# Triangular inverses with 16x16 diagonal blocks on VectorE, and cross-attention head by head, in a two-block transformer kernel

## The chip, the cores and the metric

One core of a Trainium2 chip runs the whole kernel in one launch. The metric is the device time of one execution in microseconds (us), as the median of several runs; smaller is better. Engines: TensorE (PE), VectorE (DVE), ScalarE (ACT), GpSimd (POOL) and SyncE (SP), which only issues loads and stores here.

## The reference

Two transformer blocks are applied to 256 tokens of width 2048, all in float32. The first one (a forgetting attention, an mLSTM cell, a mixture of very many small experts) isn't touched. The second one is: RMS norm, an input projection, a gated delta rule on 8 heads of 128, an RWKV-7 recurrence on 16 heads of 64, an output projection, a cross-attention with 4 heads to 256 memory tokens, and a feed-forward net. The change touches three places in it.

The delta rule solves, for each head and chunk of tokens, a unit lower triangular system:

```
a_strict = where(strict, (kb @ k^T) * decay, 0)
sol = triangular_solve(a_strict + I, rhs, lower=True)
```

The RWKV-7 recurrence is a scan over tokens in the reference; the kernel computes it in chunks of 128 tokens, and needs the inverse of a unit lower triangular 128x128 matrix for each head and chunk as well. The cross-attention:

```
scores = einsum('bshd,bmhd->bhsm', q, k) * 128 ** -0.5
probs = softmax(scores, axis=-1)
o = einsum('bhsm,bmhd->bshd', probs, v) @ wo
```

## The kernel before

Each engine has one written-out program, and the programs meet only at semaphores (`wait_ge` and `then_inc`). There is no planner: the order of the statements of an engine's program is the order of its work. In the helper class `Own`, `tell` raises a semaphore when an instruction is done, and `done` raises it and also waits for it on the same engine. SyncE streams weight tiles of 128x2048 into a ring of four slots. ScalarE rounds each slot to its high part (`high`, L1136), VectorE subtracts to get the low part (`low`, L2057), and TensorE does three passes over the parts (L2312 to L2314).

**Inverses.** There are three calls of the inversion, c = 0 (delta rule) and c = 1, 2 (the two halves of the RWKV heads). Each call inverts 16 matrices of 128x128 at once, handled in four groups q of four matrices. `Ti` holds the inverse and `Tt` its transpose. `inverse_dve` (L1605) sets both to I minus the entries inside the 2x2 diagonal blocks. Then come levels l = 1 to 5, which join blocks of 2 to 4, 4 to 8, 8 to 16, 16 to 32 and 32 to 64. In a level GpSimd (`inverse_pool`, L555) masks out the entries between the pairs of blocks (L558). TensorE (`inverse_pe`, L2446) multiplies them by Ti in `first(q)` (L2460), ScalarE (`inverse_act`, L818) copies the result to SBUF (L828), and TensorE multiplies by Tt on either side in `then(q)` (L2468, L2470). VectorE subtracts the products from Ti and Tt (L1620, L1622). TensorE's order is first 0, first 1, then 0, first 2, then 1, first 3, then 2, then 3. A last step joins 64 to 128 with 64x64 products (L2486, L2494; VectorE L1628), and updates only Tt.

For c = 0 the matrix AM is built by 16 VectorE operations (L1757) and a masking product (L1760). TensorE turns AM, and also the decay-weighted scores that L1763 writes; ScalarE copies both out (L922, L925). VectorE weights the turned K (L1767). When Tt is done, VectorE builds the right-hand side RH (L1775), and TensorE goes on (L2601). For c = 1 and 2, VectorE masks 16 products (L1990) into GR, ScalarE adds an off-diagonal part (L1099), TensorE turns the 16 matrices (L2763), and VectorE copies them out (L1994) before it starts. TensorE goes on at L2775.

**Cross-attention.** TensorE computes the scores of all heads (L2651). VectorE takes the row maxima of all in one instruction (L1848) and scales them. ScalarE does eight exponentials with sums (L990). VectorE multiplies by the reciprocal sums (L1852). TensorE turns the weights (L2657), ScalarE copies them out (L995), TensorE multiplies by the values (L2662), ScalarE copies the result (L998) and rounds it to the high part (L1000), VectorE forms the low part (L1854). Only then do ScalarE and VectorE split the first slot of the output projection `xo`, and TensorE goes on with it.

Of the kernel before, what the change touches and what calls it, by code (L numbers as in the profile page):

```python
# [17 lines left out]
F32 = mybir.dt.float32  # L18
# [7 lines left out]
P = 128  # L26
# [34 lines left out]
for _name, _units, _dv, _ac in UNITS:  # L61
# [16 lines left out]
                     ("dec_out", 1), ("atn_out", 4), ("at_out", 4), ("v_tok", 4), ("qs_out", 8), ("od_sq", 1),  # L78
                     ("od_root", 1), ("xa_exp", 1), ("xa_pt", 4), ("xo_high", 1)],
    "tensor_steps": [("gate_mm", 1), ("cumsum_mm", 1), ("r_mm", 1), ("qk_mm", 2), ("k_turned", 1), ("sm_turned", 2),  # L80
                     ("cp_mm", 4), ("num0_mm", 4), ("inter_mm", 4), ("num1_mm", 4), ("scores_mm", 8), ("hk_turned", 1),
                     ("l2_mm", 3), ("gc_mm", 1), ("dec_mm", 4), ("kk_gram", 4), ("qk_gram", 4), ("qd_turned", 4),
                     ("a_turned", 4), ("v_turned", 4), ("kd_turned", 1), ("xa_mm", 1), ("xa_turned", 4), ("xa_o", 4)],
# [4 lines left out]
                     ("dn_diag", 1), ("dec_arg", 1), ("a_ready", 1), ("qd_ready", 4), ("kd_ready", 1), ("xa_max", 1),  # L88
                     ("xa_p", 1)],
# [38 lines left out]
def build(nc, a, out):  # L128
    ctx = ExitStack()
    with ctx:  # L130
# [111 lines left out]
        OMU, OKA, SEL8 = SM[:, 192:218], SM[:, 218:226], SM[:, 226:240]  # L242
        SS, RS, RSTD = SM[:, 2:4], SM[:, 4:6], SM[:, 6:8]
# [106 lines left out]
        AOFS = [av(14336, 4, 4, P), av(33554, 4, 4, P), av(33554, 4, 4, P)]  # L350
        M1B = av(35602, 2, 4, P)

# [24 lines left out]
        RAM, RTI, RTT = av(0, 16, P), av(2048, 16, P), av(4096, 16, P)  # L377
# [176 lines left out]

        def inverse_pool(pool, c, At):  # L555
# [36 lines left out]
        def stage2_pool(pool, o):  # L592
# [5 lines left out]

            pool.wait_ge(*nth("at_out", 4))
            inverse_pool(pool, 0, AT_)  # L600
# [10 lines left out]
            for hf in range(2):  # L611
                pool.wait_ge(ev["decayed"], hf + 1)
                pool.wait_ge(ev["gram_out"], 16 * hf + 16)
                inverse_pool(pool, 1 + hf, GR[:, :, 0, :])
# [203 lines left out]
        def inverse_act(act, c):  # L818
# [4 lines left out]
            with act.Fori(1, 6, 1) as l:  # L823
                for q in range(4):
                    g = 4 * l + (24 * c - 4 + q)
# [4 lines left out]
            for q in range(4):  # L830
                g = 24 * c + 20 + q
# [5 lines left out]
        def stage2_act(act, o, half, freed, norm, high, highs):  # L837
# [82 lines left out]
            for n in range(4):  # L920
                act.wait_ge(*nth("qd_turned", n + 1))
                o.tell(nc.scalar.copy(flat(ATN)[:, BLK * n:BLK * (n + 1)], PP[:, n // 2, n % 2, :]), ev["atn_out"])  # L922
            for n in range(4):
                act.wait_ge(*nth("a_turned", n + 1))
                o.tell(nc.scalar.copy(flat(AT_)[:, BLK * n:BLK * (n + 1)], PQ[:, n, :]), ev["at_out"])  # L925
# [4 lines left out]
            inverse_act(act, 0)  # L930
# [55 lines left out]
            highs("xq", 0, (2, 3))  # L986
            freed(nc.scalar.copy(flat(XQ[:, 2:4, :]), half("xq", 0)))
            act.wait_ge(*nth("xa_max", 1))
            for n in range(8):
                ins = nc.scalar.activation(XP[:, n // 2, n % 2, :], PQ[:, n // 2, (n % 2) * T:(n % 2 + 1) * T], ACT.Exp,  # L990
                                           scale=QK_SCALE, bias=XST[:, 0, n:n + 1], accum_out=XST[:, 1, n:n + 1])
            o.tell(ins, ev["xa_exp"])
            for n in range(4):
# [611 lines left out]
        def inverse_dve(dve, o, v, c, A, At, Ti, Tt, ready):  # L1605
# [10 lines left out]
            with dve.Fori(1, 6, 1) as l:  # L1616
# [7 lines left out]
                for q in range(4):  # L1624
                    update(q)
# [1429 lines left out]
```

## Time and profile before

| | before |
|---|---|
| median of 3 runs | 3991.14 us (3989.09 to 3993.26) |
| the profiled execution, its own time | 3994.92 us |
| its span on the core | 3991.7 us |
| TensorE busy | 3712.8 us |
| VectorE busy | 2413.6 us |
| ScalarE busy | 1502.7 us |
| GpSimd busy | 157.9 us |

The three inversions lie at about 2565 to 2635, 2740 to 2814 and 2930 to 3004 us of the span, and the cross-attention at 3195 to 3221. A busy share is an average over the whole kernel; whether an instruction counts is read from the chain of waits in its stretch. TensorE instructions in fp32 appear as two records each where they are products, and as one where they are transposes.

### The profile page before, as it was taken

The page shows a single profiled execution, that of the slowest core. Times are in us where ns is not written, and L with a number is a line of the kernel's source. Part 1 is how long each engine was busy: PE and PEld are TensorE (multiplying, and loading weights), DVE is VectorE, ACT ScalarE, POOL GpSimd, SP SyncE. Part 2 cuts the span into 40 slices and gives each one's busy share as a digit, 9 for nine tenths or more (in the row PEclk, how much of TensorE's full clock was granted, in tenths as well). Part 3 has the DMA queues.
Part 4 walks back from the last instruction along what each step waited for, and adds up shares of the span by engine and source line. Part 5 has one row for each costly group of instructions (what it writes and reads, how often), then busy time and mean ns, then how long its engine had stood idle before and what let it go on. Part 6 is the DMA issues. An engine that isn't in the chain of part 4 may idle for free.

```text
span 3991.7 us, 54679 instructions
## 1 busy us (share of the span) xinstructions
PE 3712.8 (93%) x22418; PEld 3305.0 (83%) x22418; DVE 2413.6 (60%) x2621; ACT 1502.7 (38%) x1294; POOL 157.9 (4%) x159
## 2 busy tenths in 40 slices
PE   8996899999999999999999999777787969999998
PEld 8985699999988888888888989576676868888887
DVE  3544547977677766666666644456465445566656
ACT  3333333445434333433344433322222343343334
POOL 2000000000000000000000000122121000000000
PEclk8998899999999999999999999798787989999999
DMA  4451444556767765565554544000012425555554
GB/s 178 174 191 51 148 160 174 204 191 221 264 227 244 252 219 200 200 205 200 200 200 155 184 152 156 10 22 32 22 43 106 169 86 189 189 189 189 189 188 148
DMA packets 122889, 650.35 MB, mean 163 GB/s; under 512 B 10737, under 2 KB 43889, under 8 KB 49553
## 3 DMA queue, kind: packets, MB, share of 16 engines
q1 hardware_dynamic: 116224, 620.20, 44.5%
q0 software_dynamic: 6544, 28.44, 1.9%
q8 instruction: 89, 1.46, 0.2%
q14 instruction: 32, 0.25, 0.0%
HBM read 620.81 MB, written 27.79 MB: 162 GB/s over the span
## 4 chain that ended last, share of the span: by engine, by line
PE 87%; DVE 9%; ACT 2%; issue 1%; DMA 1%; DVEq 0%; ACTq 0%; POOL 0%; SPq 0%; PEldq 0%
PE pairs L2312 19%; PE pairs L2313 19%; PE pairs L2314 19%; PE quad L2357 12%; PE quad L2358 6%; DVE w_low L2057 2%; PE quad L2468 1%; PE pairs L2470 1%; PE quad L2398 1%; PE quad L2460 1%; PE quad L2865 1%; ACT w_high L1136 0%; PE quad L2703 0%; DVE arena L1940 0%; PE quad L2788 0%
## 5 line engine op out<-in xcount | busy, mean ns | idle before, releaser
L2057 DVE TENSOR_TENSOR w_low<-ring,w_high 128x2048 fp32r<-128x2048 f32 (+1 forms) x547 | 1253.2, 2292 | 926.8 <-ACT w_high L1136 926.3
L1136 ACT CAST w_high<-ring 128x2048 fp32r<-128x2048 f32 (+1 forms) x547 | 1039.2, 1901 | 1737.4 <-PE pairs L2314 1276.0
L2312 PE MATMUL pairs<-x_t,w_high 128*128 128x256 f32 x2592 | 745.4, 288 | 19.3 <-DVE w_low L2057 10.7
L2313 PE MATMUL pairs<-x_t,w_high 128*128 128x256 f32 x2592 | 738.8, 285 | 0.0
L2314 PE MATMUL pairs<-x_t,w_low 128*128 128x256 f32 x2592 | 738.8, 285 | 0.0
L2357 PE MATMUL quad<-x_t,w_high 128*128 128x512 f32 x1984 | 703.0, 399 | 9.9 <-DVE w_low L2057 9.9
L2312 PE MATMUL pairs<-w_high,act_high 128*128 128x512 f32 x1568 | 613.8, 391 | 10.2 <-DVE w_low L2057 6.5
L2313 PE MATMUL pairs<-w_low,act_high 128*128 128x512 f32 x1568 | 612.9, 391 | 0.0
L2314 PE MATMUL pairs<-w_high,act_low 128*128 128x512 f32 x1568 | 612.4, 391 | 0.0
L2358 PE MATMUL quad<-x_t,w_low 128*128 128x256 f32 x1984 | 558.1, 281 | 0.0
L2312 PEld LDWEIGHTS pairs<-x_t,w_high 128*128 128x128 f32 x2592 | 502.5, 194 | 22.0 <-DVE w_low L2057 11.8
L2313 PEld LDWEIGHTS pairs<-x_t,w_high 128*128 128x128 f32 x2592 | 502.6, 194 | 0.0
L2314 PEld LDWEIGHTS pairs<-x_t,w_low 128*128 128x128 f32 x2592 | 502.1, 194 | 0.0
L2357 PEld LDWEIGHTS quad<-x_t,w_high 128*128 128x128 f32 x1984 | 373.6, 188 | 102.6 <-DVE w_low L2057 10.3
L2358 PEld LDWEIGHTS quad<-x_t,w_low 128*128 128x128 f32 x1984 | 375.9, 189 | 1.1
L2312 PEld LDWEIGHTS pairs<-w_high,act_high 128*128 128x128 f32 x1568 | 295.6, 188 | 74.1 <-issue 12.0
L2314 PEld LDWEIGHTS pairs<-w_high,act_low 128*128 128x128 f32 x1568 | 295.5, 188 | 61.9
L2313 PEld LDWEIGHTS pairs<-w_low,act_high 128*128 128x128 f32 x1568 | 295.7, 189 | 60.1
L1429 DVE TENSOR_TENSOR x_res<-x_res,pairs 128x1024 f32<-128x1024 f32 x128 | 156.1, 1220 | 80.1 <-PE pairs L2314 79.1
L2312 PE MATMUL pairs<-w_high,x_t 128*128 128x512 f32 (+1 forms) x472 | 180.7, 383 | 9.5 <-DVE w_low L2057 9.5
L2313 PE MATMUL pairs<-w_low,x_t 128*128 128x512 f32 (+1 forms) x472 | 181.2, 384 | 0.0
L2314 PE MATMUL pairs<-w_high,x_t 128*128 128x512 f32 (+1 forms) x472 | 180.7, 383 | 0.0
(526 smaller groups left out, 3487.8 us busy)
## 6 DMA issues: line engine op xcount, KB each, us to landing
ring<-pu SPq DMA_DIRECT2D x128, 1024.0 KB, 4.9
ring<-pv SPq DMA_DIRECT2D x128, 1024.0 KB, 4.9
ring<-f SPq DMA_DIRECT2D x128, 1024.0 KB, 4.7
ring<-win SPq DMA_DIRECT2D x48, 1024.0 KB, 4.9
ring<-dn SPq DMA_DIRECT2D x32, 1024.0 KB, 4.9
ring<-rw SPq DMA_DIRECT2D x24, 1024.0 KB, 4.8
ring<-wout SPq DMA_DIRECT2D x16, 1024.0 KB, 4.9
ring<-wq SPq DMA_DIRECT2D x16, 1024.0 KB, 4.9
```

The lines of the kernel that those rows point to most:

```text
L1136: nc.scalar.copy(WH[s % 2][:, 0:w], flat(ring[s])[:, 0:w]).then_inc(ev["split_high"], 1)
L1429: v.tensor_tensor(X[:, :, cols], X[:, :, cols], PP[:, (UNIT0["peer"] + nb) % 2], ALU.add).then_inc(ev["dve_free"], 1)
L2057: v.tensor_tensor(WL[s % 2][:, 0:w], flat(ring[s])[:, 0:w], WH[s % 2][:, 0:w].bitcast(F32), ALU.subtract).then_inc(ev["split_low"], 1)
L2312: mm(out, stat[0], mov[0], start=start, stop=False, skip_group_check=True)
L2313: mm(out, stat[0], mov[1], start=False, stop=False, skip_group_check=True)
L2314: return mm(out, stat[1], mov[0], start=False, stop=stop, skip_group_check=True)
L2357: mm(PQ[:, m, :], wh[:, k, cols], XTB[:, :, kt, :], start=(kt == 0), stop=False, skip_group_check=True)
L2358: ins = mm(PQ[:, m, 0:T], wl[:, k, cols], XTH[:, kt, :], start=False, stop=(kt == KT - 1), skip_group_check=True)
L2398: ins = mm(PQ[:, 2 + b, t * P:(t + 1) * P], A0[:, b, t, :], B0[:, b, t, :], start=True, stop=True)
L2460: ins = mm(PQ[:, q % 2, m * P:(m + 1) * P], AOFS[c][:, q, m, :], Ti[:, 4 * q + m, :], start=True, stop=True)
L2468: mm(PQ[:, 2 + q % 2, m * P:(m + 1) * P], Tt[:, 4 * q + m, :], M1B[:, q % 2, m, :], start=True, stop=True)
L2470: ins = mm(PP[:, q % 2, 0, m * P:(m + 1) * P], M1B[:, q % 2, m, :], Tt[:, 4 * q + m, :], start=True, stop=True)
```

## The change

For c = 0, 1, 2 the 2x2 start and levels 1 to 3 go. A new VectorE function `substitute` inverts all 128 diagonal blocks of 16x16 (16 matrices with 8 blocks) at once, with one block in each partition: it transposes the 32x32 diagonal blocks in such a way that a partition holds two 16x16 blocks, picks one of them by a per-partition factor (EVEN16, built once), inverts by joining blocks of 2, 4, 8 and 16 inside the partition, and transposes the inverse and its transpose back into Ti and Tt, two of four row groups itself and two by a ScalarE copy. TensorE then does the level from 16 to 32 (its entries masked by ScalarE), the level from 32 to 64, where the product for Ti covers only the upper left 64x64, and the last step as before. Ti, Tt and the off-diagonal tile are cleared beforehand, by GpSimd (memset) or ScalarE (copies of zeros). For c = 0 the LS product goes, the weighting of K moves to ScalarE, and the weighting of the right-hand side moves ahead of the levels; for c = 1, 2 the turned copy of the matrices goes. The cross-attention is done head by head, and the split of xo's first slot moves ahead of it. The diff, cut to its core:

```diff
         def inverse_pool(pool, c, At):
-            for l in range(1, 6):
-                for q in range(4):
-                    if l >= 2:
-                        pool.wait_ge(ev["inv_m1"], 4 * l + (24 * c - 5 + q))
-                    between(q, LVA[:, l:l + 1, :])
+            for q in range(4):
+                pool.wait_ge(ev["inv_m1"], 12 * c + 4 + q - 1)
+                between(q, LVA[:, 5:6, :])
...
+            pool.wait_ge(used, SLOT0["out2"])
+            nc.gpsimd.memset(flat(AOFS[0]), 0.0).then_inc(ev["inv_off"], 1)
+            nc.gpsimd.memset(TTI, 0.0).then_inc(ev["inv_off"], 1)
+            pool.wait_ge(*nth("dec_mm", 4))
+            nc.gpsimd.memset(TI, 0.0).then_inc(ev["inv_off"], 1)
...
+        def block_cells(T_, g):
+            return T_[32 * g:32 * g + 32, :, 32 * g:32 * g + 32].rearrange("p m (b j) -> p j b m", b=2)
+
+        def inverse_act(act, o, c, At, Ti, Tt):
...
+            for g in range(4):
+                r, cols = slice(32 * g, 32 * g + 32), slice(32 * g + 16, 32 * g + 32)
+                ins = nc.scalar.mul(AOFS[c].rearrange("p q m s -> p (q m) s")[r, :, cols], At[r, :, cols], EVEN16[r, 0:1])
+            o.tell(ins, ev[f"off16_{c}"])
+            if c == 0:
+                act.wait_ge(ev["inv_off"], OFF0[c] + 3)
+            else:
+                nc.scalar.copy(Ti, rep(TRI[:, 0:P], 16))
+                o.done(nc.scalar.copy(Tt, rep(TRI[:, 0:P], 16)), ev[f"cleared{c}"])
+            for n, T_ in enumerate((Ti, Tt)):
+                act.wait_ge(*nth(f"blocks_turned{c}", n + 1))
+                for g in range(2):
+                    ins = nc.scalar.copy(block_cells(T_, g), BLKS[32 * g:32 * g + 32, :].rearrange("p (j b m) -> p j b m", j=16, b=2))
+                o.tell(ins, ev[f"blocks_out{c}"])
...
+        def substitute(dve, o, v, c, A, turned, Ti, Tt):
+            C, N = COEF[c], INV16[c]
+            o.tell(v.memset(N, 0.0), o.order)
+            for g in range(4):
+                r = slice(32 * g, 32 * g + 32)
+                ins = v.transpose(BLKS[r, :].rearrange("p (c b i) -> p c b i", c=16, b=2),
+                                  A[r, :, 32 * g:32 * g + 32].rearrange("p m (b c) -> p c b m", b=2))
+            o.done(ins)
+            C3 = C[:, 0:256].rearrange("p (c i) -> p c i", c=16)
+            pair = BLKS.rearrange("p (c b i) -> p c b i", c=16, b=2)
+            o.done(v.tensor_scalar(C3, pair[:, :, 0, :], MINUS16[:, 0:1], None, ALU.mult))
+            o.tell(v.memset(N[:, 0:256:17], 1.0), o.order)
+            o.done(v.scalar_tensor_tensor(C3, pair[:, :, 1, :], MINUS16[:, 1:2], C3, ALU.mult, ALU.add))
...
+            for n in (8, 16):
+                h, k = n // 2, 16 // n
...
+                for x in range(k):
+                    ins = v.tensor_tensor(prod[:, x], a21[:, x].unsqueeze(2).broadcast_to([P, h, h, h]),
+                                          n11[:, x].rearrange("p l j -> p j l").unsqueeze(1).broadcast_to([P, h, h, h]), ALU.mult)
+                o.done(ins)
+                o.done(v.tensor_reduce(sums.rearrange("p k i j -> p (k i j)"), prod.rearrange("p k i j l -> p (k i j) l"), AX.X, ALU.add))
+                for x in range(k):
+                    ins = v.tensor_tensor(prod[:, x], n22[:, x].unsqueeze(2).broadcast_to([P, h, h, h]),
+                                          sums[:, x].rearrange("p l j -> p j l").unsqueeze(1).broadcast_to([P, h, h, h]), ALU.mult)
+                o.done(ins)
+                for x in range(k):
+                    ins = v.tensor_reduce(n21[:, x], prod[:, x], AX.X, ALU.add)
+                o.done(ins)
...
+            for n, (T_, x) in enumerate(((Ti, N3.rearrange("p i j -> p j i")), (Tt, N3))):
+                o.done(v.tensor_tensor(spread, x.unsqueeze(2).broadcast_to([P, 16, 2, 16]),
+                                       EVEN16.unsqueeze(1).unsqueeze(3).broadcast_to([P, 16, 2, 16]), ALU.mult))
+                if n == 1:
+                    dve.wait_ge(*nth(f"blocks_out{c}", 1))
+                o.tell(v.transpose(BLKS[0:64, :], PRODS[0:64, :]), ev[f"blocks_turned{c}"])
+                for g in (2, 3):
+                    ins = v.transpose(block_cells(T_, g), PRODS[32 * g:32 * g + 32, :].rearrange("p (j b i) -> p j b i", j=16, b=2))
+                o.done(ins, ev["inv_new"])
...
-            o.done(v.tensor_tensor(AM, AM, rep(LS, 16), ALU.mult), ev["a_ready"])
...
+            substitute(dve, o, v, 0, AM, True, TI, TTI)
             dve.wait_ge(*nth("v_tok", 4))
-            o.done(v.tensor_tensor(RH, VT[:, 0], bc(DST[:, 4, 0, :], P), ALU.mult), ev["dn_rhs"])
+            o.tell(v.tensor_tensor(VT[:, 0], VT[:, 0], bc(DST[:, 4, 0, :], P), ALU.mult), ev["dn_rhs"])
+            inverse_dve(dve, o, v, 0, TI, TTI)
...
-            with pe.Fori(1, 6, 1) as l:
+            for l in range(2):
...
                 def then(q):
...
+                        if l == 0:
+                            mm(PQ[:, 2 + q % 2, m * P:(m + 1) * P], Tt[:, 4 * q + m, :], M1B[:, q % 2, m, :], start=True, stop=True)
+                        else:
+                            mm(PQ[0:64, 2 + q % 2, m * 64:(m + 1) * 64], Tt[0:64, 4 * q + m, 0:64], M1B[0:64, q % 2, m, 0:64],
+                               start=True, stop=True)
...
+            weights_turned(0)
+            for h in range(1, 4):
+                weights_turned(h)
+                values(h - 1)
+            values(3)
+            pe.wait_ge(ev["xo_low"], 4)
             second(pe, mm, "xo", (AH[0], AL[0]), SLOT0["xo"], DVE0["xo"] - 1)
```

The orders of the other two engines in the cross-attention: VectorE does maximum 0, 1, weights 0, maximum 2, weights 1, maximum 3, weights 2, low part 0, weights 3, low parts 1 to 3. ScalarE does exponentials 0, 1, turned copy 0, exponentials 2, turned 1, high part 0, exponentials 3, turned 2, high 1, turned 3, high 2, high 3.

## Rows read from the trace of the kernel before

**Rows 1.** The page, busy time, share of the span and instructions by engine.
```profile
PE 3712.8 (93%) x22418; PEld 3305.0 (83%) x22418; DVE 2413.6 (60%) x2621; ACT 1502.7 (38%) x1294; POOL 157.9 (4%) x159
```

**Rows 2.** Chain of waits, first inversion: start us, us, engine, tile and line.
```profile
2551.65 2.30 DVE arena L1760
...
2576.61 2.05 PE quad L2468 x8
...
2587.82 1.79 PE quad L2460 x16
...
2631.19 1.07 PE quad L2486 x16
...
2635.42 1.24 DVE arena L1775
...
2636.79 2.04 PE quad L2601 x16
```

**Rows 3.** Timeline of VectorE, around the first inversion: start us, busy us.
```profile
2547.39 4.22 DVE L1757 SCALAR_TENSOR_TENSOR arena<-pairs,arena 128x128 f32<-128x128 f32 x16 [1.82 <-ACT arena L917]
...
2553.97 2.48 DVE L1763 TENSOR_TENSOR arena<-quad,arena 128x512 f32<-128x512 f32 x4
...
2571.73 1.76 DVE L1611 TENSOR_TENSOR arena<-arena,constants 128x512 f32<-128x512 f32 x1
```

**Rows 4.** Chain of waits, second inversion.
```profile
2738.00 0.70 DVE arena L1990
...
2754.98 2.08 PE quad L2468 x8
...
2765.79 1.79 PE quad L2460 x16
...
2809.45 1.07 PE quad L2486 x16
...
2813.70 2.01 PE quad L2775 x16
```

**Rows 5.** Chain of waits, third inversion.
```profile
2927.70 0.70 DVE arena L1990
...
2944.68 2.08 PE quad L2468 x8
```

**Rows 6.** Windows: us, busy us by engine, PEclk (1.00 is full clock), DMA.
```profile
2750.00:2755.00 5.00, 2.09 (x9) 1.80 (x9) 4.93 (x7) 0.59 (x1) 1.55 (x2) 0.50 0.00 0
2760.00:2765.00 5.00, 5.00 (x47) 5.00 (x47) 2.24 (x4) 0.75 (x2) 2.19 (x2) 1.00 0.00 2
2825.00:2830.00 5.00, 5.00 (x25) 5.00 (x25) 0.69 (x1) 0.00 (x0) 0.00 (x0) 0.50 0.00 0
```

**Rows 7.** Groups by form: count | busy us, mean ns | idle before.
```profile
L791 ACT COPY arena<-quad 128x512 f32<-128x512 f32 x64 | 65.4, 1114 | 123.4 <-PE quad L2398 123.4
L828 ACT COPY arena<-quad 128x512 f32<-128x512 f32 x60 | 35.2, 587 | 164.7 <-PE quad L2460 164.7
L1622 DVE TENSOR_TENSOR arena<-arena,pairs 128x512 f32<-128x512 f32 x60 | 40.8, 681 | 0.0
L2151 DVE TENSOR_TENSOR arena<-quad,constants 128x32 f32<-128x32 f32 x1 | 0.2, 192 | 12.9 <-PE quad L2314 12.9
```

**Rows 8.** Chain of waits, cross-attention.
```profile
3195.66 3.74 PE quad L2651 x16
...
3199.42 2.30 DVE arena L1848
...
3201.95 3.77 ACT arena L990 x16
...
3206.04 2.30 DVE arena L1852
...
3208.39 3.68 PE pairs L2657 x16
...
3221.49 0.76 PE pairs L2312
```

More of the change, by code:

```diff
@@ L920, in stage2_act @@
             for n in range(4):
+                act.wait_ge(*nth("a_turned", n + 1))
+                o.tell(nc.scalar.copy(flat(AT_)[:, BLK * n:BLK * (n + 1)], PP[:, n // 2, n % 2, :]), ev["at_out"])
+            for n in range(4):
                 act.wait_ge(*nth("qd_turned", n + 1))
[L922 to L925, printed above, removed]
+                o.tell(nc.scalar.copy(flat(ATN)[:, BLK * n:BLK * (n + 1)], PQ[:, n, :]), ev["atn_out"])
             for n in range(4):
@@ L929, in stage2_act @@
                                       PP[:, n // 2, n % 2, :].rearrange("p (h d) -> p h d", h=4)), ev["v_tok"])
-            inverse_act(act, 0)
+            act.wait_ge(*nth("kd_turned", 1))
+            for h in range(DH):
+                ins = nc.scalar.mul(KD[:, h, :], PQ[:, h // 4, (h % 4) * P:(h % 4 + 1) * P], DST[:, 9, 0, h:h + 1])
+            o.tell(ins, ev["kd_ready"])
+            inverse_act(act, o, 0, AT_, TI, TTI)
             act.wait_ge(ev["qs_mm"], 1)
@@ L986, in stage2_act, with exps, turned, head_high @@
             highs("xq", 0, (2, 3))
+            highs("xo", 0, (0,))
             freed(nc.scalar.copy(flat(XQ[:, 2:4, :]), half("xq", 0)))
[L988 to L993, printed above, removed]
-                act.wait_ge(*nth("xa_turned", n + 1))
-                o.tell(nc.scalar.copy(flat(XPT[:, n]), PP[:, n // 2, n % 2, :]), ev["xa_pt"])
-            for n in range(4):
-                act.wait_ge(*nth("xa_o", n + 1))
-                ins = nc.scalar.copy(HID[:, n * T:(n + 1) * T], PQ[:, n, 0:T])
-            o.done(ins)
-            o.tell(nc.scalar.copy(AH[0][:, :], HID), ev["xo_high"])
+            def exps(h):
+                act.wait_ge(*nth(f"xa_max{h}", 1))
+                for n in (2 * h, 2 * h + 1):
+                    ins = nc.scalar.activation(XP[:, h, n % 2, :], PQ[:, h, (n % 2) * T:(n % 2 + 1) * T], ACT.Exp,
+                                               scale=QK_SCALE, bias=XST[:, 0, n:n + 1], accum_out=XST[:, 1, n:n + 1])
+                o.tell(ins, ev[f"xa_exp{h}"])
+            def turned(h):
+                act.wait_ge(*nth(f"xa_turned{h}", 1))
+                o.tell(nc.scalar.copy(flat(XPT[:, h]), PP[:, h // 2, h % 2, :]), ev[f"xa_pt{h}"])
+            def head_high(h):
+                act.wait_ge(*nth(f"xa_o{h}", 1))
+                o.tell(nc.scalar.copy(AH[0][:, h * T:(h + 1) * T], PQ[:, h, 0:T]), ev[f"xo_high{h}"])
+            exps(0)
+            exps(1)
+            turned(0)
+            exps(2)
+            turned(1)
+            head_high(0)
+            exps(3)
+            turned(2)
+            head_high(1)
+            turned(3)
+            head_high(2)
+            head_high(3)
             def o_squares(j):
@@ L2561, in stage2_pe @@
                     ins.then_inc(ev[e], 1)
-            pe.wait_ge(*nth("a_ready", 1))
+            for n in range(4):
+                pe.wait_ge(*nth("a_ready", n + 1))
+                for i in range(4):
+                    ins = nc.tensor.transpose(PP[:, n // 2, n % 2, i * P:(i + 1) * P], AM[:, 4 * n + i, :], ID)
+                ins.then_inc(ev["a_turned"], 1)
             for n in range(4):
@@ L2760, in rw_pe @@
             pe.wait_ge(ev["gram_out"], 16 * hf + 16)
-            for n in range(4):
-                for i in range(4):
-                    ins = nc.tensor.transpose(PQ[:, n, i * P:(i + 1) * P], GR[:, 4 * n + i, 0, :], ID)
-                ins.then_inc(ev["ram_turned"], 1)
             inverse_pe(pe, mm, 1 + hf, GR[:, :, 0, :], RTI, RTT)
-            pe.wait_ge(ev["inv_new"], 28 * (hf + 2))
+            pe.wait_ge(ev["inv_new"], 14 * (hf + 2))
             for t in range(NT):
```

230 lines of the change are left out of this document (140 added, 90 removed).

## Prediction

> **What bounds the kernel now.** I read the page first, then the chain of waits. On the page TensorE is busy for 93% of the span [rows 1]. The chain, read in the stretches that the change touches, shows two sorts of work there. In the inversions TensorE runs group after group without a gap: in the first one a level begins at 2576.61, the next at 2587.82, and the last small one at 2631.19 [rows 2]. In the cross-attention it waits: the chain goes TensorE, VectorE, ScalarE, VectorE, TensorE, one engine at a time over all four heads, from 3195.66 to 3221.49 [rows 8]. Both are wholly on the path, so what they lose ends the kernel earlier. Then the timeline of VectorE (when its inputs are there), the granted clock by windows, and the groups by form for prices.
>
> **What a level costs.** A full level is 12 groups of four fp32 128x128 products (first 4, then 4 + 4). From 2587.82 to 2631.19 there are four levels: 43.37, 10.84 each, 0.90 a group [rows 2]; in the second inversion 2765.79 to 2809.45 is 43.66, 10.9 each [rows 4]. The last level's 64x64 products show 16 records (two groups) in 1.07 us [rows 2], 0.54 a group. The last level stays as it is (about 4.2: 2809.45 to 2813.70 [rows 4]).
>
> **Removed.** Of levels 1 to 5, three go (2x2 to 16x16). The change keeps the one to 32x32 blocks whole and makes the next one shorter: 8 groups at 0.90 and 4 at 0.54 = 9.4. I compare from the moment at which TensorE begins the second half ("then") of the first level it does, since that moment waits for VectorE in both kernels. Behind that level, before: 43.4; after: 9.4. This saves 43.4 - 9.4 = 34.0 us in the first inversion and 43.7 - 9.4 = 34.3 in the second; the third repeats the second, so 34.3 too. The first level itself I take as equally long: before, 2576.61 to 2587.82 = 11.2 and 2754.98 to 2765.79 = 10.8 [rows 2, 4], of which some 2 us are a cold clock.
>
> **Added: the substitution, before that moment.** Its VectorE work is 33 instructions in one chain, nearly all with a wait for the one before. Prices: 512 elements 0.68 us (0.61 from start to start when unwaited, 0.70 when waited for), 32 elements 0.19, so 0.21 for a tiny one, about 0.3 for 128 elements, 0.42 for 256 [rows 7].
> - Collecting the blocks: 4 transposes of 32x512 (2.5), two memsets (0.4), two operations on 256 (0.8): 3.7.
> - Blocks of 2 and 4: 6 tiny ones, 1.3. Blocks of 8: 7 of 64 to 128 elements, 1.7. Blocks of 16: 4 of 512 elements, 2.8.
> - Spreading the inverse and its transpose back: each a product of 512 and three transposes, 2.6, together 5.2.
>
> Sum: 14.7 us. No row shows a VectorE transpose. From below it can't be cheaper than a plain pass of 512 elements. From above: 11 of the 512-element instructions read or write single words far apart, and so do the ScalarE copies. A ScalarE copy that writes words 128 bytes apart takes 1.11 us where a plain one takes 0.59 [rows 7]. With this 0.53 on all 11, and 0.5 for the last copies, T is 21.0. I take the dear price for the scattered writes alone (4 VectorE transposes into Ti and Tt, 2.1, and 0.3 for the last ScalarE copies), since the row is one of a write and no row shows a dear read: **T = 17.1**, with 14.7 and 21.0 kept as ends.
>
> The Trainium skill, "SBUF — State Buffer", section on the ports ("SBUF cachelines"), speaks against this change: accesses that leave a 16-byte line each time pay a penalty, reads as well as writes. By that rule T would lie at the upper end, 21.0, and the time 12 us above my sum; it is a rival below. The same skill's "VectorE: DVE Perf Modes", section "The three transpose paths", has 311 ns for a bf16 VectorE transpose of 128 columns; four times that, an estimate, would be 1.24 us for 512 and T near 20.
>
> Where T starts: in the second and third inversion with the last mask product of VectorE, 2738.00 + 0.70 and 2927.70 + 0.70 [rows 4, 5], because the diagonal blocks no longer need TensorE's turned copy. So "then" begins at 2738.70 + 17.1 = 2755.8 instead of 2754.98 and 2945.5 instead of 2944.68: 0.8 later each. In the first, after L1757 and L1763 but without the LS product (2.30): 2547.39 + 4.22 + 2.48 = 2554.1 [rows 2, 3], plus 17.1 = 2571.2 instead of 2576.61: 5.4 earlier. There the product for RH (2635.42 to the start of TensorE at 2636.79 [rows 2]) moves beside the levels: 1.2 more.
>
> **Hidden.** ScalarE gets the decay-weighted K (8 small ones), the four masked products and, in the second and third, two clearing copies of 2048. All of it ends by about 8.5 us after T starts, and Ti is first wanted 10 us after. If that cover went, each us late would count. GpSimd loses 16 of 20 masked products per inversion and gets memsets that lie before; beside such a mask product a VectorE SBUF product of 512 took 1.76 us, not 0.68 [rows 3], as I read it because of GpSimd, so less of them costs nothing. Three tiny VectorE operations (EVEN16) in the stage's start: 0.6 lost at most.
> The clock: while VectorE substitutes, TensorE is idle, and its granted clock is 0.50 (1.2 GHz) at 2750 and 1.00 (2.4 GHz) again from 2760, some 4 us after it runs without a gap [rows 6]. Before, it fell in the same place. After, the two "first" groups run cold beside the end of the substitution, so the cost is about the same, within 1 us each way per inversion.
>
> Inversions: 34.0 + 5.4 + 1.2 = 40.6; 34.3 - 0.8 = 33.5 twice. Together 107.6.
>
> **Cross-attention head by head.** Before: scores 3.74, maximum 2.30 and a small one, exponentials 3.77, weighting 2.30, turning 3.68 to 3212.07, then values, copies, the high and low parts and the split of xo's first slot, and TensorE at 3221.49 [rows 8]. After, a quarter of each: scores 0.93, maximum and scaling 0.9 (0.68 for 512 elements and a tiny one), exponentials 0.95, weighting 0.9 (a tiny one and two of 256, started one behind the other), turning 0.5 at full clock (3.68 / 4 is 0.92 at the halved one), copy 0.6 (the plain ScalarE copy of 512), and for values, high and low part, each an estimate from the prices of 256 elements, 0.9, 0.4 and 0.4. I walked the written order: head 0's weights are ready at 3199.7; VectorE and ScalarE alternate; maximum 3 ends at 3202.4, exponentials 3 at 3204.2, weights 3 at 3205.1, turned and copied at 3206.2, values 3 (behind values 2) at 3207.4, its low part at 3208.3. The split of xo's first slot now lies beside the last slot of xq, where both engines idle. TensorE starts xo at 3208.5: **13.0** less. If TensorE also keeps the full clock, up to 2 more (it begins xo after long idling before, and needs some 4 us at half speed after such idling, as in the inversions); if the hops cost more, down to 0.
>
> **Sum.** 107.6 + 13.0 - 0.6 = 120.0. Against the profiled execution: its span 3991.7 becomes 3871.7, its time 3994.92 becomes 3874.9. The median of the runs is 3991.14, 3.8 below the profiled one, which gives 3871.1. I forecast **3872 us**. T at its ends gives 3865 and 3884.
>
> **Rivals.**
> 1. *Scattered words are dear everywhere on VectorE, or a transpose is dearer than a pass.* For: the ScalarE row, and no row of the new operation. Against: the VectorE groups that I read cost a plain pass, but none has its SBUF words so far apart. T = 21 to 24, 4 to 7 us more per inversion: 3884 to 3893.
> 2. *The clock stays down through the levels*, since half of the shorter level's and all of the last one's products use a quarter of the array. For: at 2825 to 2830 TensorE was busy for all 5 us, with products of 64 columns, and was granted 0.50 [rows 6]. Against: the last level, all 64x64, took 0.54 a group at full clock before. The 22.6 us of levels would double, less the 2 already cold: 20 more each, 3932.
> 3. *The cross-attention keeps its length*, its gain eaten by the hops between engines (4 heads, 7 hops): 3885.
> 4. *Slower than before*: the substitution on one engine costs more than the three levels. TensorE would idle where it now works. The saving of 120 is gone when T is 57, that is 40 us more, which over the 11 scattered instructions is 3.6 us on each, 4.3 us for 512 elements. From there it is slower; at 5 us each, T = 65 and 3991 + 24 = 4015. Against: the slowest row of 512 elements on VectorE that I found is the 1.76 us above [rows 3].
> 5. *The change doesn't do what it says*: TensorE still waits for something else at "then" (ScalarE's clearing copies, or GpSimd's memset). Their sum above leaves 2 us of room; if ScalarE were 5 us late in each, 3887.
>
> **Chances.** Forecast (3858 to 3880) 0.62; rival 1 0.23; rival 3 0.05; rival 5 0.04; rival 2 0.04; rival 4 0.02. The range is 3858 to 3893: below the plain T with a warmer clock (3865 less 2 for xo and 1 per inversion is 3860), above T = 24. It leaves out rivals 2 and 4 and part of the others. A measurement of this kernel tells about 0.2% (8 us) from no change. Faster by more 0.97, within it 0.01, slower 0.02.
>
> **What would show it.** In the trace after: per inversion one full level of 10.8 to 11.5, one of 9.4, one of 4.2; between the last mask product and the first "then" 17 us; VectorE transposes of 0.6 when plain and 1.2 when they write Ti or Tt; ScalarE's clearing copies over before VectorE's spreading begins; from TensorE's last xq pass to the first of xo about 14 us, not 27. I am wrong if T is outside 14.7 to 21, if the granted clock is at 0.50 through the second level, or if TensorE waits for ScalarE or GpSimd, not VectorE, at the start of the levels.

## The result

The changed kernel takes 3877.3 us (median of 4 runs, 3873.0 to 3878.7) beside 3992.2 us for the kernel before (4 runs): ratio 0.9712, 95% interval 0.9695 to 0.9728. The forecast was 3872, range 3858 to 3893. Its profiled execution took 3878.63 us with a span of 3876.7, against 3994.92 and 3991.7: 115.0 us of span less, where the sum of the prediction said 120.0.

The page, engines (busy time, share, instructions; answers to [rows 1]):

```profile
PE 3597.7 (93%) x21522; PEld 3187.8 (82%) x21522; DVE 2369.5 (61%) x2611; ACT 1508.0 (39%) x1293; POOL 101.7 (3%) x116
```

The chain of waits, first inversion (start us, us, engine, tile, line; answers to [rows 2]). L1668 is the first instruction of the substitution, L2616 the first "then", L2605 x16 the first two groups of the second level, L2637 the last level:

```profile
2555.61 0.28 DVE arena L1668
...
2574.86 0.60 ACT arena L864
2575.50 1.16 PE quad L2616 x8
...
2584.70 1.79 PE quad L2605 x16
2586.48 0.60 PE quad L2618 x8
2587.09 1.09 PE pairs L2621 x8
...
2595.04 1.07 PE quad L2637 x16
```

The same of the second inversion [rows 4]:

```profile
2701.08 0.70 DVE arena L2135
...
2721.66 1.31 PE quad L2616 x8
...
2745.60 2.01 PE quad L2933 x16
```

Two levels and the short last one stand where five and the last one stood, and T, from the substitution's start (or the mask product's end) to "then", is 19.9 us in both. The experiments below count T from the first instruction of the substitution in all three inversions; so counted, the changed kernel has 19.9, 19.8 and 19.8.

VectorE's timeline in the first inversion (the operation, output and input shapes, count):

```profile
2555.82 4.17 DVE L1671 STREAM_TRANSPOSE arena<-arena 32x512 f32<-32x512 f32 x4
...
2561.14 0.17 DVE L1692 TENSOR_TENSOR arena<-arena 128x8 f32<-128x8 f32 x1
...
2564.74 0.69 DVE L1708 TENSOR_REDUCE arena<-arena 128x64 f32<-128x512 f32 x1
2565.47 1.07 DVE L1710 TENSOR_TENSOR arena<-arena 128x512 f32<-128x512 f32 x1
...
2567.29 1.01 DVE L1723 TENSOR_TENSOR arena<-arena,constants 128x512 f32<-128x512 f32 x1
2568.34 0.70 DVE L1727 STREAM_TRANSPOSE arena<-arena 64x512 f32<-64x512 f32 x1
2569.07 2.08 DVE L1729 STREAM_TRANSPOSE arena<-arena 32x512 f32<-32x512 f32 x2
2571.18 0.69 DVE L1723 TENSOR_TENSOR arena<-arena,constants 128x512 f32<-128x512 f32 x1
```

Equal amounts of work have two prices: 0.69 to 0.70 us where the words lie side by side (L1708, L1727, the second L1723), 1.01 to 1.07 where they are read or written far apart.

The cross-attention, chain of waits [rows 8]: 12.7 us from the scores to xo's first pass, instead of 25.8.

```profile
3094.30 1.15 PE quad L2802 x4
...
3106.99 0.50 PE pairs L2452
```

The ledger, in us of the span, from milestones in the two traces:

| stretch | forecast | measured |
|---|---|---|
| stage ahead of the first inversion | +0.6 | +1.5 |
| first inversion | -40.6 | -39.0 |
| second, third | -33.5 each | -31.2, -31.9 |
| cross-attention, to xo's first pass | -13.0 | -13.1 |
| xo's first passes at full clock | 0 to -2 | -2.1 |
| all else | 0 | +0.8 |

### The profile page after: what moved, and what is told of

Read it like the earlier page. It is cut to its first block, busy times and chain, and to the rows that moved or that the text cites. A ratio compares the mean times of both kernels' runs of the same rounds, so it can differ in the third digit from the quotient of the medians.

```text
span 3876.7 us, 52423 instructions
## 1 busy us (share of the span) xinstructions
PE 3597.7 (93%) x21522; PEld 3187.8 (82%) x21522; DVE 2369.5 (61%) x2611; ACT 1508.0 (39%) x1293; POOL 101.7 (3%) x116
## 4 chain that ended last, share of the span: by engine, by line
PE 86%; DVE 10%; ACT 2%; issue 1%; DMA 1%; DVEq 0%; ACTq 0%; POOL 0%; SPq 0%; PEldq 0%
PE pairs L2452 20%; PE pairs L2453 19%; PE pairs L2454 19%; PE quad L2497 12%; PE quad L2498 6%; DVE w_low L2197 2%; PE quad L2538 1%; PE quad L3023 1%; PE pairs L2621 1%; ACT w_high L1195 0%; PE quad L2605 0%; PE quad L2865 0%; PE quad L2946 0%; PE quad L2947 0%; DMA arena<-xaw 0%
## 5 line engine op out<-in xcount | busy, mean ns | idle before, releaser
L2452 PE MATMUL pairs<-x_t,w_high 128*128 128x256 f32 x2592 | 743.7, 287 | 19.9 <-DVE w_low L2197 11.2
```

The costliest lines, as they stand in the source:

```text
L2452: mm(out, stat[0], mov[0], start=start, stop=False, skip_group_check=True)
```

## The experiments

Unless said otherwise, "the changed kernel" is 3877.3 us. Kernels were timed beside the kernel before, which had medians of 3992.8 to 3993.5.

**Cross-attention undone.** VectorE's, ScalarE's and TensorE's orders of the cross-attention are those of the kernel before:

```
-            row_max(0)
-            row_max(1)
-            shares(0)
...
+            o.done(v.tensor_reduce(XST[:, 0, :]..., PQ[:, :, :]..., AX.X, ALU.max))
+            o.done(v.tensor_scalar(XST[:, 0, :], XST[:, 0, :], -QK_SCALE, None, ALU.mult), ev["xa_max"])
```

> The three inversions are as after the change; the cross-attention is as before it. Theory: the traces put 13.1 us of the gain between the start of the scores and the first pass of xo, another 2.1 us in xo's first passes (full clock at once, where the kernel before ran its first 11 passes at the halved clock), and about 0.8 us are given back later. So this kernel should take 14.5 us more than the changed one: 3891.8 us, with 25.8 us from scores to xo. Rival: the inversions alone bring the gain and the cross-attention only moves waits about: 3877 to 3880.

Measured: 3891.9 us (3887.0 to 3893.2), ratio to before 0.9742 [0.9725, 0.9758]. The theory holds; the two parts of the change add up.

**The split alone.**

```
             highs("xq", 0, (2, 3))
+            highs("xo", 0, (0,))
...
-            highs("xo", 0, (0, 1, 2))
+            highs("xo", 0, (1, 2))
```

> The inversions as after; the cross-attention over all heads at once as before it, but with the split of xo's first slot moved ahead of it. Theory: in the kernel before, the low part of the attention's output is done at 3218.55 and TensorE starts at 3221.49, so the split is worth 2.9 us and the rest of the 14.5 is the work head by head: 3888.9. Rival: the split is what TensorE waited for, and head by head brings little: 3880 or less.

Measured: 3888.9 (3885.7 to 3890.6). The 3.0 us between the two medians lie within the spread of either, but they are what the row of 2.9 us says; that head by head brings the larger part (11.6) is beyond the spread. The chain of its profile agrees: 23.0 us from the scores to xo's first pass (3094.52 to 3117.56), where the kernel before has 25.8 and the changed one 12.7.

**The second level in full width.**

```
-                        if l == 0:
-                            mm(PQ[:, 2 + q % 2, m * P:(m + 1) * P], Tt[...], M1B[...])
-                        else:
-                            mm(PQ[0:64, 2 + q % 2, m * 64:(m + 1) * 64], Tt[0:64, ..., 0:64], M1B[0:64, ..., 0:64])
+                        mm(PQ[:, 2 + q % 2, m * P:(m + 1) * P], Tt[...], M1B[...])
```

> The product for Ti in the second level covers all 128x128 again. The trace of the changed kernel shows 10.34 us for this level, with 64x64 products at 0.60 a group and the 128-wide group behind each at 1.09 instead of 0.90. Theory (changing between the two sizes costs 0.2 each time): the level becomes a full one of 10.84, 0.5 more each, 3878.8. Rival (my forecast of 9.4 for the short level was right and something else in it takes 0.9): 1.4 more each, 3881.6.

Measured: 3878.1 (3875.8 to 3881.1). From the first "then" to the last "then" group of the second level the changed kernel took 18.4 us in the first inversion; this one 18.9 (2574.18 to 2593.09); the other two inversions show 0.4 more. So the short product is worth 0.4 to 0.5 us in each, and the difference in the medians (0.8 us) lies within the spread.

**Without the small products.**

```
-                    for m in range(4):
+                    for m in range(4 if l == 0 else 0):
```

> The four groups of 64x64 products for Ti in the second level are left out (Ti isn't updated there). Theory (they cost their own 0.60 and 0.20 more in the group behind them): the level falls from 10.34 to 7.2, 3.1 each, 3867.9. Rival (the group behind is slow for a reason of its own, such as waiting for a copy): only 2.4 or less each, 3870 or more.

Measured: 3869.2 (3869.0 to 3870.2). Its timeline of TensorE, second level (L2605 "first", L2617 the wide groups of "then"):

```profile
2581.84 1.95 PE L2605 MATMUL quad<-arena 128*128 128x128 f32 x16
2583.62 1.10 PE L2617 MATMUL pairs<-arena 128*128 128x128 f32 x8
2584.56 1.06 PE L2605 MATMUL quad<-arena 128*128 128x128 f32 x8
2585.46 1.06 PE L2617 MATMUL pairs<-arena 128*128 128x128 f32 x8
```

Group follows group after 0.9 us again, and the level takes 7.3 us (2581.84 to 2589.17). Four groups of 64x64 cost 3.1 us: 0.60 each, and the rest in the group behind each.

**Adjacent words on VectorE.**

```
-                ins = v.transpose(BLKS[r, :]..., A[r, :, 32 * g:32 * g + 32].rearrange("p m (b c) -> p c b m", b=2))
+                ins = v.transpose(BLKS[r, :]..., A[r, 0:4, :])
...
-                    ins = v.transpose(block_cells(T_, g), PRODS[...])
+                    ins = v.transpose(T_[32 * g:32 * g + 32, 0:4, :], PRODS[...])
```

> Every VectorE instruction of the substitution that reads or writes words far apart (4 transposes that collect, 4 that write Ti and Tt, 3 products of 512 elements) does as much work on adjacent words, so the wrong elements are inverted. ScalarE's copies stay. In the changed kernel these take 1.01 to 1.08 us and plain ones of the same size 0.69 to 0.70. Theory (the distance is the price, whatever the operation): 0.36 less on each of the 11, of which the last two lie beside ScalarE's copies (2.15 us) and bring little: T from 19.9 to 16.6 to 17.0, 3.1 each, 3868. Rival (a transpose of 32 rows is dear in itself): only the 3 products get cheaper, 1.1 each, 3874.

Measured: 3870.3 (3866.5 to 3870.5). T is 17.3, 16.9 and 16.9. The rival (3874, only the products cheaper) is excluded: the transposes fell too. Its timeline of VectorE, first inversion:

```profile
2555.00 2.80 DVE L1671 STREAM_TRANSPOSE arena<-arena 32x512 f32<-32x512 f32 x4
...
2561.40 1.02 DVE L1704 TENSOR_TENSOR arena<-arena 128x512 f32<-128x512 f32 x1
2562.45 0.69 DVE L1707 TENSOR_REDUCE arena<-arena 128x64 f32<-128x512 f32 x1
2563.17 0.69 DVE L1709 TENSOR_TENSOR arena<-arena 128x512 f32<-128x512 f32 x1
...
2566.08 1.42 DVE L1728 STREAM_TRANSPOSE arena<-arena 32x512 f32<-32x512 f32 x2
```

A transpose of 32x512 costs 0.70 when both sides are adjacent: it is not dear in itself. L1704 stayed at 1.02 in the first inversion, where its other operand is still read in turned order; that is the 0.4 us by which T is longer there.

**And on ScalarE.**

```
-                    ins = nc.scalar.copy(block_cells(T_, g), BLKS[...])
+                    ins = nc.scalar.copy(T_[32 * g:32 * g + 32, 0:4, :], BLKS[...])
```

> As the kernel with plain words on VectorE, and ScalarE's four block copies write adjacent words too. A plain ScalarE copy of 512 elements takes 0.59, these 1.05. Theory: ScalarE is what is late at the end of the substitution once VectorE is faster, so this takes another 0.9 us off each: T about 15.9, 3865.5. Rival (VectorE still ends last): no difference to the kernel with VectorE alone.

Measured: 3863.2 (3861.9 to 3864.0); T 16.3, 16.1, 16.1. ScalarE was late next, as expected, by 0.8 to 0.9 us. The time fell by 7.0, not by the 2.6 that T gives: in its profile the substitution of the first inversion starts 1.9 us earlier, though nothing ahead of it differs, and its first "then" groups ran at full clock where the kernel above had them at half (1.0 us). Such differences are the subject of the next experiments.

**TensorE kept at work.**

```
+            if c:
+                pe.wait_ge(ev["gram_out"], 16 * c)
+            for _ in range(46 if c == 0 else 68):
+                mm(PP[:, 1, 1, 0:P], ID, ID, start=True, stop=True)
             for l in range(2):
                 def first(q):
```

> TensorE does 46 or 68 products of 128x128 (one in 0.22 us, the results unused) while VectorE substitutes, so it is not idle and its clock should stay at full speed. Theory (the halved clock falls on the two first groups, which wait for nothing that matters, since the copy behind them waits for ScalarE's block copies until the same moment): at most 0.5 us less in all, 3876.8, with a granted clock of 1.00 at first. Rival (the cold clock costs what I took, 1 to 2 us in each inversion): 3872 to 3874.

Measured: 3878.1 (3875.8 to 3879.6): no gain, as the theory had it, but for a reason more. In the first inversion the idle products ended last: "first" began behind them at 2567.58 and "then" right behind it, 20.0 us after the start. In the second and third they ended in time. TensorE's timeline in the second inversion (L2595 idle products, L2609 "first", L2620 "then"; in brackets the pause before and who ended it), then windows (us, busy us and instructions by engine, granted clock, DMA):

```profile
2696.29 15.42 PE L2595 MATMUL pairs<-constants 128*128 128x128 f32 x136 [2.06 <-ACT arena L1158]
2711.95 2.02 PE L2609 MATMUL quad<-arena 128*128 128x128 f32 x16 [0.24 <-ACT arena L855]
2715.94 2.08 PE L2620 MATMUL quad<-arena 128*128 128x128 f32 x8 [1.97 <-ACT arena L864]
```

```profile
2712.00:2714.00 2.00, 1.97 (x16) 1.78 (x16) 1.94 (x3) 0.90 (x1) 0.74 (x1) 1.00 0.00 0
2714.00:2716.00 2.00, 0.06 (x1) 0.06 (x1) 1.21 (x2) 1.95 (x4) 1.76 (x2) 0.99 0.00 0
2716.00:2718.00 2.00, 2.00 (x9) 2.00 (x10) 0.00 (x0) 0.37 (x1) 0.00 (x0) 0.50 0.00 0
```

The first groups now take 2.0 us instead of 3.75, so TensorE is done with them 2 us before ScalarE's copy (L864), pauses, and begins "then" at the halved clock. The two levels take 1.5 us longer for it. In the changed kernel the slow first groups fill just this pause. The median alone would not show this: in this profile the first substitution starts 6.1 us earlier than in the changed kernel's (2549.55, not 2555.61), in a stage that is the same, and the chain behind the second inversion, also the same, is 5.0 us longer.

**Packed blocks, one spreading product.**

```
+            for n, (T_, form) in enumerate(((Ti, "p (j b i) -> p i b j"), (Tt, "p (j b i) -> p j b i"))):
...
+                dve.wait_ge(*nth(f"packed{c}", 14))
+                ins = v.transpose(BLKS, PRODS)
...
+                if m >= 3 and m % 2 == 1:
+                    n = m // 2 - 1
+                    for g in ((0, 1) if n % 2 == 0 else (2, 3)):
+                        o.tell(pack(nc.scalar.copy, GR[:, :, 0, :], g, n // 2), ev[f"packed{1 + hf}"])
```

> A version meant to be better, same result. ScalarE packs the diagonal blocks into adjacent words ahead of the substitution (for c = 0 two of four row groups, for c = 1 and 2 all but the last piece, which VectorE does), so the collecting transposes become one plain one for c = 1, 2 (0.70 and about 0.6 for the last piece, not 4.17) and one plain and two far apart for c = 0 (2.8). One product spreads the inverse for both Ti and Tt, 0.7 less; the order of the 512-element product is turned so that its second operand is adjacent, 0.35 less. Theory: T 2.4 less for c = 0, 3.7 less for c = 1 and 2, 3867.5. Rival (ScalarE's packing delays the products that precede the second and third inversion, or reading far apart in the spreading transposes costs more than 0.36): half of it or less, 3872.

Measured: 3874.4 (3872.7 to 3877.2), 7 us more than forecast. T is 17.6, 16.6 and 16.6, close to what was expected, and the mask products ahead of the inversion are not delayed. Of the 7 us, T accounts for 1.1, the first inversion's two levels, begun at the halved clock, for 0.9, and the chain behind the second inversion for 3.8; the rest is open. TensorE's timeline there, the packed kernel and below it the changed one (the same three steps of the recurrence, 8 and twice 16 products):

```profile
2759.14 2.05 PE L2954 MATMUL quad<-arena 128*128 128x128 f32 x8 [0.94 <-DVE arena L2175]
2760.98 3.52 PE L2957 MATMUL quad<-arena 128*128 128x64 f32 x16
2765.35 3.68 PE L2962 MATMUL quad<-arena 128*128 128x64 f32 x16 [0.86 <-DVE arena L2168]
```

```profile
2763.78 1.13 PE L2930 MATMUL quad<-arena 128*128 128x128 f32 x8 [0.94 <-DVE arena L2151]
2764.75 1.90 PE L2933 MATMUL quad<-arena 128*128 128x64 f32 x16
2767.50 2.00 PE L2938 MATMUL quad<-arena 128*128 128x64 f32 x16 [0.85 <-DVE arena L2144]
```

The two longer groups do the same work in twice the time: the halved clock in this chain takes back 3.8 us that the shorter substitution had won.

**One spreading product alone.** The part of the packed kernel that starts with `for n, (T_, form)`, and the turned order of the product.

> One part of the packed version alone: one product spreads the inverse for Ti and Tt, and the order of the 512-element product is turned; the collecting transposes are as in the changed kernel. The packed version gained 2.3, 3.2 and 3.2 us in T by the trace, but only 2.9 us in time; in its profile the chain that follows the second inversion ran at the halved clock where the changed kernel's ran at full clock, 3.8 us longer. Theory: T falls by 1.05 in each inversion, 3874.1, if the chains behind keep the clock they had; where the clock falls in one of them, up to 3.8 more, 3878. Rival (the traces' durations don't add up to time): no change in T.

Measured: 3874.1 (3869.8 to 3875.3); T is 18.9, 18.8 and 18.8, 0.9 less each. The stretch behind the second inversion was 1.1 us longer in its profile than in the changed kernel's.

**Packed, idle products without a pause.**

```
+            idle(54 if c else 34)
...
                 first(1)
+                if l == 0:
+                    idle(6)
                 then(0)
```

> The packed version with idle products of TensorE (34 for c = 0, 54 for c = 1, 2 ahead of the first groups, and 6 between the first groups and the second half), so it doesn't pause there. The earlier kernel with idle products paused for 1.97 us behind the first groups, and its level then began at the halved clock and took 1.4 us more. Theory (the pause is what let the clock fall): from the second half of the first level to the last level 19.5 us in all three, against 20.3, 19.8 and 19.4, and T as in the packed version: 1.1 us less than it, 3873.3, or 3869.5 if the chain behind the second inversion runs at full clock again. Rival: the clock falls with or without the pause, same time as packed.

Measured: 3877.5 (3870.5 to 3878.5), not the 3873.3 of the theory. The levels did become 19.4 to 19.5 us from "then" to the last level in all three: without a pause the clock stayed up. But I had put in too many idle products. For c = 0 and 1 they began at the halved clock and held up "first" by 4.2 and 1.2 us, and "then" came 21.4 and 17.3 us after the start, not 17.6 and 16.6. The chain behind the second inversion was 3.8 us longer again.

**Idle products in the recurrence too.**

```
                 ins.then_inc(ev["rx_mm"], 1)
+                idle(6)
                 pe.wait_ge(ev["rx_out"], n)
...
                 ins.then_inc(ev["sa_mm"], 1)
+                idle(6)
                 pe.wait_ge(ev["sa_out"], n)
```

> As packed_warm, with 6 idle products (0.67 us at full clock) also in each wait of TensorE in the chains behind the second and third inversion (three waits for each of two tiles, 0.85 to 0.94 us each). In the changed kernel's trace the granted clock is 0.50 for about 20 us of these chains, though TensorE's gaps are no longer than that. Theory (filling the gaps keeps the clock at 1.00): the interval from the end of the second inversion to the next substitution falls from 117.6 us by up to 7, the same behind the third: 3858. Rival (the clock falls in these chains for another reason than the gaps, since it stays down while TensorE works without a gap on products of 64 columns): the idle products take 1.34 us at the halved clock where the gap is 0.85, 0.5 us more in each of 12 waits, 3878.

Measured: 3852.8 (3848.4 to 3853.8), ratio to before 0.9648 [0.9635, 0.9661]: 24.5 us less than the changed kernel. Windows in the recurrence, the changed kernel and below it this one:

```profile
2750.00:2754.00 4.00, 3.15 (x16) 2.96 (x15) 0.69 (x1) 0.00 (x0) 4.00 (x2) 0.50 0.00 0
2754.00:2758.00 4.00, 4.00 (x20) 4.00 (x21) 0.00 (x0) 0.00 (x0) 1.36 (x1) 0.50 0.00 0
2758.00:2762.00 4.00, 4.00 (x21) 4.00 (x21) 0.69 (x1) 0.00 (x0) 0.00 (x0) 0.50 0.00 0
```

```profile
2746.00:2750.00 4.00, 4.00 (x38) 4.00 (x37) 0.63 (x1) 0.00 (x0) 2.99 (x1) 1.00 0.02 4
2750.00:2754.00 4.00, 4.00 (x38) 4.00 (x38) 0.75 (x2) 0.00 (x0) 0.00 (x0) 1.00 0.00 0
2754.00:2758.00 4.00, 4.00 (x38) 4.00 (x38) 0.69 (x1) 0.00 (x0) 0.00 (x0) 1.00 0.00 0
```

TensorE was busy for all 8 us from 2754 in the changed kernel and was granted half the clock; what differs is that it had paused 0.85 us here and there before. With the pauses filled, the clock stays at 1.00, and from the last wide group of the second inversion to the next substitution it is 109.4 us (2733.82 to 2843.23), not 118.7; from the third substitution to the scores 221.8, not 235.4, of which 3.2 are the shorter T. The fair comparison is the kernel above, which differs in these idle products alone: 3877.5 to 3852.8, 24.7 us. In the two profiles the chain behind the second inversion is 13.1 us shorter and the stretch from the third substitution to the scores 10.2.

The expectation had the price of the idle products wrong. Six of them take 1.34 us at full clock, not 0.67 (L2960 idle products, L2977 the next step; VectorE's result, which that step waits for, from its own timeline):

```profile
2741.06 1.56 PE L2960 MATMUL pairs<-constants 128*128 128x128 f32 x12
2742.45 1.90 PE L2977 MATMUL quad<-arena 128*128 128x64 f32 x16
```

```profile
2741.33 0.69 DVE L2168 TENSOR_SCALAR arena<-quad 128x512 f32<-128x512 f32 x1 [2.16 <-PE quad L2971]
```

The result is there at 2742.02, and the step begins at 2742.45. From step to step it is 3.23 us (from 2739.22), where the changed kernel at full clock took 2.85 (2745.60 to 2748.45). So each filled wait is overrun by some 0.4 us, and the kept clock gains far more than that. Whether three or four idle products would keep the clock as well was not tried.

**A better version.** Fewer idle products ahead of "first", and more in the stage ahead of the first inversion:

```
-            idle(54 if c else 34)
+            idle(48 if c else 12)
...
+            idle(30, PQ[:, 3, :])
             pe.wait_ge(*nth("dn_sq", 1))
...
+            idle(14, PQ[:, 3, :])
             pe.wait_ge(*nth("l2_inv", 1))
```

> As packed_keep (3852.8 us), with fewer idle products ahead of the first groups (12 instead of 34 for c = 0, where the first groups began 4.2 us late behind them, 48 instead of 54 for c = 1, 2), and with idle products in three waits of TensorE ahead of the first inversion (30 in 7.5 us, 14 in 3.7 us, 8 in 3.1 us), where the trace shows a granted clock of 0.50 in most of the work that follows. Theory: the start of the substitution of c = 1 comes 3.8 us earlier by the shorter T of c = 0, that of c = 2 another 0.7; the sums of squares fall from 8.8 to 6.7 us, the spreading of the roots from 13.0 to 7: together 12 to 13 us, 3840. Rival (the clock in that stage follows another cause than the gaps): only the 4.5 us of the two T, 3848.

Measured: 3844.3 (3841.8 to 3845.8), ratio to before 0.9629 [0.9616, 0.9642], 33.0 us less than the changed kernel. T is 17.5, 16.5 and 16.6. TensorE's timeline in that stage (L2722 sums of squares, L2730 spreading the roots, L2717 idle products):

```profile
2504.26 7.08 PE L2722 MATMUL quad<-arena,constants 128*16 128x256 f32 x32 [0.84 <-ACT arena L946]
2511.27 3.39 PE L2717 MATMUL quad<-constants 128*128 128x128 f32 x28
2515.08 5.35 PE L2730 MATMUL quad<-arena,constants 16*128 16x256 f32 x16 [0.42 <-DVE arena L1871]
2520.22 7.03 PE L2730 MATMUL pairs<-arena,constants 16*128 16x256 f32 x16
```

```profile
2511.00:2515.00 4.00, 3.66 (x30) 3.20 (x28) 1.72 (x1) 3.52 (x5) 0.00 (x0) 1.00 0.00 0
2515.00:2518.00 3.00, 2.92 (x11) 2.48 (x12) 0.02 (x1) 2.97 (x5) 0.00 (x0) 0.83 0.02 5
2520.00:2524.00 4.00, 4.00 (x10) 3.13 (x10) 2.29 (x1) 0.56 (x1) 0.00 (x0) 0.50 0.00 0
```

The squares fell to 7.1 us, but the roots only fell from 12.8 to 12.2: L2730 began at 1.00 and dropped to 0.50 while TensorE worked without a gap on products that read 16 partitions. The granted clock was still 1.00 from 2516 to 2517 and was 0.50 from 2517 to 2518. In the kernel before this one the clock also fell to 0.50 within 2 us of the roots' start, although TensorE had paused 3.7 us ahead of them and not 0.4. There the rival was right: filling the pause did not keep the clock. That the 16 partitions are the cause is not shown, since no run changed them. The 5 us that the roots did not give are more than the 4 us by which the forecast was missed; the product behind the third filled wait, which went from 6.4 to 3.6 us, made up for a part.

## Why the prediction was right, step by step

**Right in mechanism and size.** The removed levels (10.84 each); the last level (4.2); TensorE waiting for VectorE, not for ScalarE's clearing copies or GpSimd, at "first"; the cross-attention (13.0 forecast, 13.1 to the first pass; shown by undoing it); rivals 2, 3 and 4 did not come about. Part of the nearness of the total is luck: T and the short level alone would have made it 11.2 us too low, and a gain in the first level that the sum did not have took back 5.0 of it.

**T, 17.1 forecast, 19.9 measured: the term of the sum that was mis-sized, +2.8 in each inversion.** I took the dear price for scattered writes alone, since the one row of it was a write. Reads turned out as dear: the four collecting transposes took 4.17 us where I had 2.5 (+1.7), and three products 1.01 to 1.07 instead of 0.68 (+1.0). The scattered writes cost 0.36 more than a plain instruction, not 0.53 (4 x 0.17 = -0.7). The last 0.7 us is a wait for ScalarE (rival 5, in small; I had put 0.3 there): its copy for "then" (L864, 2574.86) stands behind its four block copies and also waits for VectorE's last transpose; both end at 2574.8, so "then" begins 0.7 us after VectorE's last transpose. Some 0.4 is spread over the hand-overs between the small instructions. Rival 1 had the right cause, and its lower end was 21 because it used 0.53. The experiment with adjacent words shows the cause of the first two by taking it away.

The Trainium skill, "SBUF — State Buffer" ("SBUF cachelines"), has every access that crosses to a new line pay a penalty. The traces agree, for reads as for writes. The measured price is 0.32 to 0.38 us on 512 elements. The estimate of 1.24 us for a transpose, worked out from the Trainium skill, "VectorE: DVE Perf Modes", section "The three transpose paths", is refuted: a plain one of 32x512 or 64x512 took 0.70.

**The short level, 9.4 forecast, 10.34 measured.** I took 0.54 a group from the last level, where 64x64 follows 64x64. Between wide groups a small one takes 0.60, and the wide one behind it 0.2 more than in a run of wide ones. Both the full-width kernel and the one without small products show it. The Trainium skill, "TensorEngine Tiling (Array Packing)", section "Key Properties", says that changing the tiling mode drains the engine; the trace agrees, with 0.2 us a change.

**The first level, taken as equally long (11.2 and 10.8), measured 9.2 and 9.35.** Before, "then" stood 2.64 us after the first groups and began at the halved clock. Now the two first groups (3.75 us, at the halved clock) end 0.25 us ahead of "then", and the clock rises with it:

```profile
2571.49 3.75 PE L2605 MATMUL quad<-arena 128*128 128x128 f32 x16 [12.55 <-ACT arena L855]
```

The halved clock moved beside the substitution; I had written that its cost would stay the same within 1 us, and it fell by 1.5 to 2.0. The kernel kept at work shows the other side: a pause of 1.97 us in this place costs 1.5.

**The stage ahead, +0.6 forecast, +1.5 measured.** It can't be put down to the three small operations. Nine kernels whose code is the same up to there start the first substitution between 2549.6 and 2555.9 us, with the granted clock at other places in the stage. One profile can't settle 1 or 2 us here, in either direction, nor can it in the chain behind the second inversion: from the start of the last level to the next substitution it is 117.5 to 117.6 us in seven profiles and 118.6 to 122.5 in four, of kernels whose TensorE code is the same there (in two of the four ScalarE packs blocks in this stretch).

So the sum came out at 115 of 120: T -8.4, the short level -2.8, against +5.0 from the first level, +2.1 in xo, and about -1 for the rest.

## What to carry to other kernels

Price a VectorE or ScalarE instruction by how its words lie, on both sides, before counting instructions; and count a small TensorE product by its neighbours. When an engine replaces work of TensorE's, ask what the clock does in the new pause: a pause under 1 us, repeated, was enough here to halve the clock for the work behind it, and idle products in it gave 24.7 us although each wait was overrun by some 0.4. Where they overran the need by 4.2 us, or left a pause of 2 us behind them, they gained nothing.

## What the runs showed of the hardware

- VectorE, 512 elements in each partition: 0.69 adjacent, 1.01 to 1.08 where one side's words are far apart; the same for a transpose, and no more with both sides far apart (the packed kernel's transposes that read and write so took 1.05 each). A ScalarE copy of 32x512: 0.63 and 1.05.
- TensorE's clock fell to half in a chain with pauses of 0.85 to 0.94 us, and stayed down through 8 us without a pause, mostly on products of 64 columns; with the pauses filled the same products ran at full clock. It also fell within 2 us of the start of products that read 16 partitions, with a pause of 0.42 us ahead of them and, in another kernel, one of 3.74.
- Idle products of 128x128 in fp32 take 0.22 us each at full clock (six in 1.34).
- Groups of 64x64 between groups of 128x128 cost 0.78 us each, counted with what they add to the group behind, for half the columns and a quarter of the array; a wide group costs 0.90.
